# Low halves of the second phase's weight tiles: from GpSimd to VectorE

## What is computed

```python
h   = rmsnorm(x) * (1 + sc1) + sh1
mix = concat(hgrn2(h @ w_in), mamba2_ssd(h @ w_in), rwkv7(h @ w_in)) @ w_out
x   = x + g1 * mix
h   = rmsnorm(x) * (1 + sc2) + sh2
x   = x + g2 * ((silu(h @ w_gate) * (h @ w_up)) @ w_down)
y   = rmsnorm(x)
```

## Time and profile before

| | us |
|---|---|
| median of 3 runs | 1834.2 (1832.74 to 1850.1) |
| the profiled execution | 1846.01 |
| its span on the core | 1844.2 |
| PE busy, share of the span | 1623.2, 88% |
| DVE busy | 1046.7, 57% |
| ACT busy | 660.3, 36% |
| POOL busy | 251.9, 14% |
| mean granted TensorE clock | 0.923 |

### The profile page before, as it was taken

One profiled execution on the slowest core, in us unless ns is written; L12 is line 12 of the kernel. 1 busy time (PEld: TensorE's weight loads), 2 busy tenths in 40 slices (PEclk: granted clock), 3 DMA queues, 4 the chain that ended last, 5 costly groups with the idle time before them and its releaser, 6 DMA issues.

```text
span 1844.2 us, 32572 instructions
## 1 busy us (share of the span) xinstructions
PE 1623.2 (88%) x13599; PEld 1477.5 (80%) x13599; DVE 1046.7 (57%) x2159; ACT 660.3 (36%) x1131; POOL 251.9 (14%) x331
## 2 busy tenths in 40 slices
PE   4799999879999766786988799999899999999995
PEld 2798888768888633475877799999899999999995
DVE  5513455676545365677667344576665556655554
ACT  2313333133233322333433244334444444433332
POOL 4411111111110120232333310100000000000000
PEclk9899999888899866787988899999999999999998
DMA  8111001110111244511222344444464535564451
GB/s 311 52 46 35 24 24 31 36 39 32 43 47 36 95 135 155 163 59 54 61 64 64 107 149 126 133 131 128 130 181 151 158 116 149 147 177 135 144 145 64
DMA packets 276426, 188.07 MB, mean 102 GB/s; under 512 B 7823, under 2 KB 264320, under 8 KB 275256
## 3 DMA queue, kind: packets, MB, share of 16 engines
q1 hardware_dynamic: 265602, 159.48, 29.0%
q0 software_dynamic: 7728, 23.27, 3.8%
q10 hardware_dynamic: 2950, 3.24, 0.5%
HBM read 172.82 MB, written 13.18 MB: 101 GB/s over the span
## 4 chain that ended last, share of the span: by engine, by line
PE 69%; DVE 17%; ACT 8%; issue 4%; DMA 2%; SPq 0%; POOL 0%; DVEq 0%; ACTq 0%; POOLq 0%
PE bank L1321 17%; PE bank L1322 17%; PE bank L1323 17%; PE bank L1257 3%; ACT WHI L1899 2%; DVE WLO L2373 1%; PE bank L1549 1%; PE bank L1548 1%; PE bank L1494 1%; PE bank L1487 1%; PE bank L1496 1%; PE bank L1343 1%; PE bank L1663 1%; PE bank L1431 1%; DMA ADAW<-in_w_ada 1%
## 5 line engine op out<-in xcount | busy, mean ns | idle before, releaser
L2373 DVE TENSOR_TENSOR WLO<-RAW,WHI 128x1024 fp32r<-128x1024 f32 (+4 forms) x235 | 247.1, 1052 | 268.2 <-ACT WHI L1899 266.5
L1899 ACT CAST WHI<-RAW 128x1024 fp32r<-128x1024 f32 (+4 forms) x294 | 266.3, 910 | 228.3 <-PE bank L1323 202.2
L1321 PE MATMUL bank<-HAH,WHI 128*128 128x384 f32 (+1 forms) x832 | 277.8, 334 | 10.1 <-DVE HAL L2554 4.6
L1322 PE MATMUL bank<-HAL,WHI 128*128 128x384 f32 (+1 forms) x832 | 274.0, 329 | 0.0
L1323 PE MATMUL bank<-HAH,WLO 128*128 128x384 f32 (+1 forms) x832 | 273.7, 329 | 0.0
L1321 PE MATMUL bank<-HHI,WHI 128*128 128x344 f32 x568 | 192.1, 338 | 10.7 <-DVE HLO L2590 6.6
L1073 POOL TENSOR_TENSOR WLO<-RAW,WHI 128x1024 fp32r<-128x1024 f32 (+1 forms) x59 | 125.0, 2121 | 455.3 <-ACT WHI L1899 455.3
L1322 PE MATMUL bank<-HLO,WHI 128*128 128x344 f32 x568 | 185.5, 327 | 0.0
L1321 PE MATMUL bank<-MIXR,WHI 128*128 128x384 f32 (+2 forms) x528 | 174.0, 330 | 12.9 <-DVE MIXR L2503 3.8
L1323 PE MATMUL bank<-HHI,WLO 128*128 128x344 f32 x568 | 185.2, 326 | 0.0
L1321 PEld LDWEIGHTS bank<-HAH,WHI 128*128 128x128 f32 x832 | 160.5, 193 | 14.2 <-issue 13.4
(11 more groups left out here) (569 smaller groups left out, 2842.8 us busy)
## 6 DMA issues: line engine op xcount, KB each, us to landing
RAW<-in_w_gate SPq DMA_DIRECT2D x66, 512.0 KB, 4.0
RAW<-in_w_up SPq DMA_DIRECT2D x66, 512.0 KB, 4.0
RAW<-in_w_ada SPq DMA_DIRECT2D x32, 512.0 KB, 4.2
RAW<-in_w_in SPq DMA_DIRECT2D x26, 512.0 KB, 3.9
RAW<-in_w_out SPq DMA_DIRECT2D x24, 512.0 KB, 3.6
RAW<-in_w_down SPq DMA_DIRECT2D x32, 384.0 KB, 3.2
RAW<-in_w_down SPq DMA_DIRECT2D x32, 320.0 KB, 2.9
ADAW<-in_w_ada SPq DMA_DIRECT2D x8, 1024.0 KB, 20.3
```

The costliest lines, as they stand in the source:

```text
L1321: mm(bank[:, 0:w], whi[:, k, :], hi_k, start=(k == 0), stop=False)
L1322: mm(bank[:, 0:w], whi[:, k, :], lo_k, start=False, stop=False)
L1899: a.copy(w_split(i)[0][:, 0:nk, :], RAW[u % NRAW][:, 0:nk, :]).then_inc(w_hi, 1)
L2373: v.tensor_tensor(wlo[:, 0:nk, :], RAW[u % NRAW][:, 0:nk, :], whi[:, 0:nk, :].bitcast(F32), ALU.subtract).then_inc(w_lo, 1)
```

## The change

The splits of phase 2 that stand ahead of the `mark` in the plan, 42 of them (26 with 8 k-tiles, 16 with 4), had `LO_BY` = `pool`; now all splits of phase 2 have `dve`. POOL skips them, and DVE issues `split_lo(i)` where the plan has `('split', i)`: it waits for the cast and makes the low half, ahead of whatever follows in the plan. Phase 1 keeps its assignment; slots, loads, casts and matmuls stay as they are.

```diff
         if ffn[0][0] == 'stop':
             ffn.pop(0)
-        samples_at = len(PLAN2)
         PLAN2.append(('mark', 0))
         fill(10, True)
...
-        for at, (what, arg) in enumerate(PLAN2):
+        for what, arg in PLAN2:
             if what == 'split':
-                LO_BY[arg] = 'pool' if at < samples_at else 'dve'
+                LO_BY[arg] = 'dve'
```

## The result

The changed kernel takes 1860.5 us (median of 4 runs, 1859.1 to 1864.5) against 1833.5 for the kernel before: a ratio of 1.0137, 95% interval 1.0108 to 1.0166. Measured once more beside others (run after_again) it is 1.0155 (1.0132 to 1.0178). So it is slower by 25 to 29 us. The forecast was +15.6 us (1850 us), with 1835 to 1867 as its range; the loss is 10 to 13 us larger than forecast.

What follows compares the result with a forecast made beforehand. The bound was taken to be the ping-pong between PE, ACT and DVE in each block, not POOL's slowness. Idle +12.2 and clock +3.4 made +15.6 us on the 1834.2 median: 1850 us, range 1835 to 1867.

Steps and rivals of the forecast that it cites:

- rival 1: Same mechanism, but the clock's upper price holds or DVE falls a step further behind: 1858 to 1872 us, chance 0.24.
- Slower by over 1%: Whole kernel: the case of a time more than 1% over the kernel before, above 1852.5 us, chance 0.44.
- within 1%: Whole kernel: the case of a time from 1816 to 1852.5 us, chance 0.50.
- start of block 3: Start of block 3: HAD's copies, no longer held up by GpSimd, end sooner, so PE idles 3.2 us less.
- HT and T: Blocks 3, 5, 6, 7: low halves delay both HGRN2's and Mamba's output squares; PE idles 9.7 us more.
- HKT: Blocks 4 to 7: DVE's clamp or eviction and squares, behind low halves, delay the copy PE awaits: +6.0 us.
- down units and the first of the mark: Down units, 1030 to 1070 us: MIXR comes 1.1 later, waits for POOL's low halves go; sum -0.3 us.
- clock: PE in the blocks: added idle lowers the granted clock, 0.28 us per us of idle, +3.4 us for 12.2.
- Order decides, not the sum: DVE in the blocks: 39.5 us added against 32.7 given back hardly changes its total; the order of work decides.
- 32.7: DVE in the stretch: us lost in 19 rows held up by GpSimd's low halves, counted as given back.
- The upper bound of the prediction: Clock price from above: each of four new HT waits costs 2.8 us, like the costliest row; 11.4 in all.
- Rival 3: DVE on the chain, freed from GpSimd's blocking, gains 14.9 us, 19 with the clock: about 1815 us, chance 0.06.

Runs made afterwards that it cites:

- after_again: The changed kernel, unaltered, measured once more beside other runs on the same chip: 1862.8 us, ratio 1.0155 to the kernel before.
- again: The kernel before, unchanged, run once more for a second profile: ratio 0.9991, profile span 1836.8 us.
- defer: The changed kernel with each low half of the blocks moved later in DVE's order, past evictions and listed vector work: 1827.3 us, ratio 0.9947.
- thin_dve: The changed kernel with the 42 low halves on DVE cut to 2 of 128 columns per k-tile, waits and order kept: 1838.9 us, ratio 1.0011.
- ht_back: The changed kernel with five of the 42 low halves, those between a filler and HT, given back to GpSimd: 1853.2 us, ratio 1.0081.
- hkt_back: The changed kernel with four low halves, ahead of the clamp or eviction before HKT, given back to GpSimd: ratio 1.0084.
- warm_again: Second measurement of the changed kernel with 20 discarded matmuls ahead of PE's wait for HT in blocks 3, 5, 6, 7: 1851.4 us, ratio 1.0093.
- thin_pool: The kernel before with the 42 low halves on GpSimd cut to 2 of 128 columns per k-tile: 1810.7 us, ratio 0.9855.

## Why the prediction was right, and what was mis-sized

The mechanism and the direction came as forecast, step by step. The size did not: 1860.5 us is inside the range (1835 to 1867), but above the 1841 to 1858 that the prediction gave its own forecast, and in the reach of rival 1, the same mechanism with a dearer clock (1858 to 1872, chance 0.24). "Slower by over 1%" had 0.44, less than the 0.50 of "within 1%". That the range holds the time is owed to its width. The steps against the profiles of run again and of the changed kernel (us of PE's wait, or of time):

| step | forecast | measured |
|---|---|---|
| start of block 3 | -3.2 | -3.4 (HAL 4.7, now a low half 1.3) |
| HT and T | +9.7 | +10.4 (HT +14.9, T -4.5) |
| HKT | +6.0 | +6.9 |
| down units and the first of the mark | -0.3 | +1.6 (MIXR +1.4, XTB +2.6, POOL's low halves -1.9, XTA -0.5) |
| sums before the norm (SSA) | none | +0.4 |
| all waits | +12.2 | +15.9 |
| clock | +3.4 | +8.0 (5.9 busy time in the blocks, 2.1 behind); +10.3 in after_again (8.3, 2.0) |

- **The bound and the order.** POOL's slowness was not the bound; this reading held. "Order decides, not the sum" held in that the same work at another place is 35 us faster (defer). But the work is not free: each low half's own 1.2 us stands in the chain behind the cast, and thin_dve prices this at 23 to 26 us with the clock. DVE's busy time in the stretch grew by 11.9 us (6.8, which is 39.5 less 32.7, had been forecast), in part because the small low halves take 0.69 us and not 0.6, and because the 4.3 us given back at the copies to HAD lie ahead of the stretch.
- **HT and T.** HT 4.1 us late in block 3 was forecast, 4.03 measured; block 5 was 3.36 later (3.71 in all) against 3.3, block 6 3.76 against 3.9, block 7 3.70 against "3 to 4". ACT's squares held T up as walked, and T's waits in blocks 6 and 7 shrank. HT and T together grew by 4.5, 3.5, 0.6 and 1.7 us in blocks 3, 5, 6 and 7, against +4.5, +3.3, +0.3 and +1.6. ht_back confirms the link.
- **HKT.** 1.6 late in block 5 was forecast, 1.86 measured (1.87 to 3.73); hkt_back confirms it.
- **Down units.** Here a step is missing. I counted MIXR (+1.1, measured +1.4) and the end of POOL's waits, but not that the last copy of x on DVE (XTB) now stands behind a low half, while PE's first unit of the mark waits for all copies of x: a wait of 2.6 us, where PE had waited 1.15 for POOL's low half. The earlier trace rows could not show it, since it was no wait then. The rule would have been to name, for each item behind a low half, who waits for it; I did that for the blocks and not for the items x.
- **Clock.** This is the term that was mis-sized: 3.4 against 8 to 10. I laid the slow units on all idle time alike, 0.28 us for each. But the new waits for HT are not spread; each is 3.7 to 4.0 us long, and in blocks 3, 5 and 6 a filler unit follows almost at once. These three units took 4.46, 4.46 and 4.44 us in run again, 4.67, 4.98 and 5.78 in the changed kernel, and 6.18, 6.11 and 5.04 in after_again. The units behind HKT, whose waits grew from 0.8 to 3.2 us to 2.7 to 4.5, took 21.9 us together in run again and 24.7 in the changed kernel. And the first unit of the mark, behind the wait for XTB, took 5.98 us where it had taken 4.40; this is most of the 2.1 behind the blocks. Which of the old units are slow changes between profiles of one kernel with the same waits (the unit behind T in block 3 took 4.98 us in the first profile and 6.44 in run again), so no single unit prices a wait. The upper bound of the prediction (11.4) was nearer, and rival 1 with it. warm_again shows the size by filling the idle time at four places without taking a dependency away: 7.4 us at those places, 11 in the medians.
- **The port freed.** Rival 3 priced the relief at 19 us with the clock; thin_pool, which has it alone with next to none of the work on POOL, gives 26 (22 to 31). The mechanism was real, and the 32.7 us nearly so (for the same 427 instructions from the copies to HAD on, DVE's busy time fell by 28.9 from the first profile to thin_pool's), and the Trainium skill's page "SBUF — State Buffer" (Who interferes with whom) is borne out. What the change lost was not this gain but its cover: 26 us of relief, 28 of waiting for the cast and about 24 of work in the wrong place make +26; each of the three holds the clock that goes with it, and each is known to some 4 us.
- **Not settled.** 3.6 us of PE idle that the profile puts down to "issue" differ between the two profiles in blocks 0 to 3 (7.6 against 4.0). They hide part of the loss in the span's sum and are not the change's: in after_again they are 7.0. Runs of the kernel before, side by side, differ by up to 20 us (1822.9 to 1843.1), which no run here explains.

## What to carry to other kernels

When work is moved to an engine that issues in order, first ask what it waits for there, not how long it takes: a low half of 1.2 us that must wait for a cast after the filler took DVE away from work that had run under the filler. Write the moved step into the new engine's own order, behind everything that is ready earlier and ahead of its own deadline; that one reordering turned +1.4 or +1.5% into -0.5% (defer). And price a new wait ahead of a run of matmuls at well over its length, since the clock falls with it.

## What the hardware did that I had not expected

Eighty matmuls of useless work made the kernel 11 us faster (warm_again against after_again), because the matmuls behind stayed at a higher granted clock: 0.87 in the mean of the stretch against 0.84. And GpSimd's long low halves cost the kernel before some 26 us in all (thin_pool), with 1.9 us of them visible as a wait of PE for GpSimd: the rest was in DVE rows that were merely longer than their like, and in the clock behind the waits that they lengthened.
